# An encoder layer's modulation, projections and attention, reordered

## What is computed

```
mod = silu(c) @ w_ada[l] + b_ada[l]            # 1024 x 6144, six vectors of 1024
h = rms_norm(x, norm1_g[l]) * (1 + sc1) + sh1
z = h @ w_in[l]                                # za 512, zb 768, zq 512, zk 512, zv 512
ya = silu(rms_norm(conv31(val * sigmoid(gate))))   # za: val, gate: the A group
yb = rms_norm(bg * conv3(cg * hv))                 # zb: bg, cg, hv: the B group
yc = diff_attention(zq, zk, zv)                # 4 heads; two softmaxes per head, subtracted
x = x + g1 * (concat(ya, yb, yc) @ w_out[l])
h = rms_norm(x, norm2_g[l]) * (1 + sc2) + sh2
x = x + g2 * ((silu(g) * u) @ w_down[l])       # g, u = halves of h @ w_gate_up[l]
```

## Time and profile before

| | |
|---|---|
| runs (3) | 1303.79, 1305.12, 1305.97 us; median 1305.12 |
| the profiled execution | 1303.42 us, span 1301.7 |
| TensorE busy | 1200.7 us, 92% |
| VectorE, ScalarE, GpSimd busy | 751.9, 459.6, 133.2 us |
| DMA | 158.39 MB, mean 122 GB/s |

### The profile page before, as it was taken

How to read it: one execution, slowest core, us unless ns; L and a number is a source line. 1 busy time by engine, 2 the same in 40 slices (tenths; PEclk the granted TensorE clock), 3 DMA queues, 4 the chain that set the end, 5 groups by cost and what they waited for, 6 DMA issues and landing times.

```text
span 1301.7 us, 14677 instructions
## 1 busy us (share of the span) xinstructions
PE 1200.7 (92%) x5232; PEld 946.1 (73%) x5232; DVE 751.9 (58%) x962; ACT 459.6 (35%) x687; POOL 133.2 (10%) x175
## 2 busy tenths in 40 slices
PE   0799877898999999999999999689899999999999
PEld 0588653486888888888887886337688888888887
DVE  5889988577766433345556898773543333332321
ACT  2323249834322222222224223694332222222220
POOL 6572000031000000001111000001200000000000
PEclk9899999998999999999999999899999999999999
DMA  9552131054766222255552322101222222223232
GB/s 365 188 186 102 65 95 67 1 215 157 247 224 207 85 94 98 95 207 196 194 195 79 97 81 81 49 1 49 81 86 96 95 98 95 96 96 110 100 113 81
DMA packets 39208, 158.39 MB, mean 122 GB/s; under 512 B 4528, under 2 KB 4672, under 8 KB 39040
## 3 DMA queue, kind: packets, MB, share of 16 engines
q1 hardware_dynamic: 29664, 105.02, 24.0%
q0 software_dynamic: 9504, 52.84, 10.8%
HBM read 155.75 MB, written 2.10 MB: 121 GB/s over the span
## 4 chain that ended last, share of the span: by engine, by line
PE 70%; DVE 17%; ACT 5%; POOL 3%; DMA 2%; issue 2%; DVEq 0%; ACTq 0%; SPq 0%; POOLq 0%
PE ps L1174 20%; PE ps L1175 20%; PE ps L1176 20%; DVE uc L880 4%; PE ps L1198 3%; DVE w_lo L804 3%; DVE ada_acc_early L821 2%; PE ps L1346 2%; PE ps L1202 1%; ACT prob L740 1%; DVE ada_acc_first L821 1%; DMA ada_ring_first<-ada 1%; PE ps L1213 1%; DVE neg_max L1061 1%; DMA raw<-w_stream 1%
## 5 line engine op out<-in xcount | busy, mean ns | idle before, releaser
L547 ACT ACTIVATE w_hi<-raw 128x1024 fp32r<-128x1024 f32 x196 | 207.3, 1060 | 674.3 <-PE ps L1176 537.5
L804 DVE TENSOR_TENSOR w_lo<-raw,w_hi 128x1024 fp32r<-128x1024 f32 x196 | 240.8, 1231 | 291.3 <-ACT w_hi L547 289.4
L1174 PE MATMUL ps<-h_hi,w_hi 128*128 128x512 f32 x896 | 349.8, 390 | 0.0
L1176 PE MATMUL ps<-h_lo,w_hi 128*128 128x512 f32 x896 | 349.0, 390 | 0.0
L1175 PE MATMUL ps<-h_hi,w_lo 128*128 128x512 f32 x896 | 349.0, 389 | 0.0
L1174 PEld LDWEIGHTS ps<-h_hi,w_hi 128*128 128x128 f32 x896 | 168.3, 188 | 35.1 <-DVE w_lo L804 0.4
L1176 PEld LDWEIGHTS ps<-h_lo,w_hi 128*128 128x128 f32 x896 | 168.3, 188 | 34.8
L1175 PEld LDWEIGHTS ps<-h_hi,w_lo 128*128 128x128 f32 x896 | 168.3, 188 | 34.6
L1174 PE MATMUL ps<-gu_hi,w_hi 128*128 128x512 f32 x352 | 137.4, 390 | 0.0
L1176 PE MATMUL ps<-gu_lo,w_hi 128*128 128x512 f32 x352 | 137.1, 390 | 0.0
L1175 PE MATMUL ps<-gu_hi,w_lo 128*128 128x512 f32 x352 | 137.1, 390 | 0.0
(11 more groups left out here) (172 smaller groups left out, 1260.0 us busy)
## 6 DMA issues: line engine op xcount, KB each, us to landing
raw<-w_stream SPq DMA_DIRECT2D x196, 512.0 KB, 3.3
ada_ring_late<-ada POOLq DMA_DIRECT2D x16, 768.0 KB, 8.2
ada_ring_first<-ada POOLq DMA_DIRECT2D x12, 768.0 KB, 17.0
ada_ring_gu_hi<-ada POOLq DMA_DIRECT2D x10, 768.0 KB, 5.7
ada_ring_gu_lo<-ada POOLq DMA_DIRECT2D x10, 768.0 KB, 5.1
ada_ring_early<-ada POOLq DMA_DIRECT2D x8, 768.0 KB, 10.1
ada_ring_conv<-ada POOLq DMA_DIRECT2D x4, 768.0 KB, 7.8
xT<-x_t POOLq DMA_DIRECT2D x1, 2048.0 KB, 13.8
```

The costliest lines, as they stand in the source:

```text
L547: act.activation(w_hi[:, u % RING, :], raw[:, u % RAW, :], ACT.Copy).then_inc(s_whi, 1)
L804: dve.tensor_tensor(w_lo[:, u % RING, :], raw[:, u % RAW, :], w_hi[:, u % RING, :].bitcast(F32), ALU.subtract).then_inc(s_wlo, 1)
L1174: pe.matmul(dst, whi, rhs[0][:, n, :], start=start, stop=False)
L1176: return pe.matmul(dst, whi, rhs[1][:, n, :], start=False, stop=stop)
```

## The change

- **Modulation.** w_ada is laid out with its output features on the partitions, so a chunk is one DMA of 512 KB, and its 128 values are row sums: one VectorE operation multiplies 1024 elements by silu(c), which is broadcast over the partitions (`c_b`), and accumulates (`mod_dot`). There are 96 such modulation rows, numbered in the order of use: 0 to 15 are shift and scale 1 of layer 0, from 16 (M_MID) on three for each chunk (gate 1, shift 2, scale 2), from 40 (M_GU) on 28 in gate-up and from 68 (M_DOWN) on 28 in down. TensorE's column sums are gone. Rings hold 8 or 4.
- **Start.** x comes first, in four DMAs of SyncE; the rows follow on GpSimd. The first norm's squares lie in eight buffers and TensorE adds all of them. VectorE computes the angles. Shift and gain of a chunk are made as soon as its two dots are (`first_gain`, on ScalarE).
- **Order.** Units run A (4), K (4), Q (4), V (4), B (6). A and K units hold two chunks of h each; in layer 0 they alternate, chunk by chunk (`a_chunk`, `k_chunk`), in layer 1 A comes before K.
- **B in attention.** A half of a B unit (12 matmuls, `b_half`) stands before the tiles and in each of tiles 0 to 10. Part of the taps (48 operations in layer 0, 26 in layer 1) and the short convolution move to the tiles.
- **Output.** Three units instead of two are taken chunk by chunk, in an order of chunks by layer, and seven banks are in use.

```diff
+N_AK, N_Q, N_V, N_B, N_OUT, N_GU = 8, 4, 4, 6, 8, 2 * FC
...
+A_AT = ((0, 2, 4, 6), (0, 1, 2, 3))
+K_AT = ((1, 3, 5, 7), (4, 5, 6, 7))
...
+TAPS_UNIT = ({9: 1, 10: 2, 13: 1, 14: 2, 15: 1}, {3: 2, 4: 3, 5: 3, 6: 3, 9: 1, 10: 2, 13: 1, 14: 2, 15: 1})
+TAPS_TILE = ([2] * 12, [2] * 6 + [1])
...
+            pool.wait_ge(s_x[1], 16)
+            for m in range(2):
+                ada_load(m)
...
+            pool.wait_ge(s_scores, N_TILES)
+            for m in range(M_MID + 4, M_MID + 8):
+                ada_load(m)
+            for k in range(KC - 1):
+                norm_sum(1, k)
+                for m in range(M_MID + 8 + 3 * k, min(M_MID + 8 + 3 * (k + 1), M_GU)):
+
+                    pool.wait_ge(s_acc, m - 8 + 1)
+                    ada_load(m)
+
+            pool.wait_ge(s_acc, M_GU)
...
+            def first_gain(k):
+
+                act.wait_ge(s_acc, 2 * k + 2)
+                a = mod_at(SH1, k)
+                act.activation(mod[:, 0, a:a + 1], modr[:, 0, a:a + 1], ACT.Identity,
+                               bias=pcol[:, 0, C_BADA + a:C_BADA + a + 1]).then_inc(s_gain0, 1)
+                act.activation(gain[:, 0, 0, k:k + 1], modr[:, 0, a + 1:a + 2], ACT.Identity,
+                               scale=pcol[:, 0, C_N1 + k:C_N1 + k + 1],
+                               bias=n1b[:, k:k + 1]).then_inc(s_gain0, 1)
...
-            def mod_load(G, q, i=0):
-
-                slots, acc = ada_place(G)
-                ada_landed(dve, G, q, i)
-                if q == 0 and G >= FIRST_MG:
-
-                    dve.wait_ge(s_msum, G + i if G in GU_MG else G - 1)
-                for r in range(2):
-                    k = 2 * q + r
-                    src = slots[q][:, r, :]
-                    if k == 0:
-                        dve.tensor_scalar(acc, src, c_act[:, k:k + 1], None, ALU.mult).then_inc(s_acc, 1)
-                    else:
-                        dve.wait_ge(s_acc, 8 * G + k + 8 * i)
-                        dve.scalar_tensor_tensor(acc, src, c_act[:, k:k + 1], acc, ALU.mult,
-                                                 ALU.add).then_inc(s_acc, 1)
...
+            def mod_dot(m):
+
+                ada_landed(dve, m)
+                l, a = divmod(m, MODS)
+                slot = ada_slot(m)
+                dve.scalar_tensor_tensor(slot, slot, 1.0, c_b[:], ALU.mult, ALU.mult,
+                                         accum_out=modr[:, l, a:a + 1]).then_inc(s_acc, 1)
...
+            mod_dot(0)
+            mod_dot(1)
+            dve.wait_ge(s_nrs, 1)
...
+                if l == 0:
+                    for k in range(KC):
+                        dve.wait_ge(s_gain0, 2 * k + 2)
+                        norm_apply(0, 0, k)
+                        if k < 2:
+                            split_lo(2 * k)
+                        elif k + 1 < KC:
+                            mod_dot(2 * k + 2)
+                        norm_lo(0, 0, k)
+                        if k < 2:
+                            mod_dot(2 * k + 2)
+                        if k + 1 < KC:
+                            mod_dot(2 * k + 3)
+                        if k < 2:
+                            split_lo(2 * k + 1)
+                        elif k % 2:
+                            split_lo(k + 1)
+                            split_lo(k + 2)
+                    first = 6
...
+                    taps = TAPS_TILE[l][it] if it < len(TAPS_TILE[l]) else 0
+                    conv_a_taps(l, taps // 2)
+                    row_factors(l, it)
                     if it:
-                        row_mix_in(it - 1)
-                    if 2 <= it < 2 + 2 * CC:
-                        y_lo(l, it - 2)
-                    h, r = divmod(it - 2 * NT, NT)
-                    if h >= 1 and r == 0:
-                        mix_scale(l, 3 + h)
-                    if h >= 1 and r == 3:
-                        y_lo(l, 3 + h)
-                row_mix_in(N_TILES - 1)
+                        row_mix_in(l, it - 1)
+                    for k in range(len(SCALE_AT[l])):
+                        if SCALE_AT[l][k] == it:
+                            mix_scale(l, k)
+                    if it in (2, 6):
+                        short_input(l, it // 4)
+                    if it in (3, 7):
+                        short_conv(l, it // 4)
+                    if it in (8, 10):
+                        short_gate(l, (it - 8) // 2)
+                    conv_a_taps(l, taps - taps // 2)
+                    if it % 2 == 0 and it < 2 * N_B:
+                        split_lo(U + U_B + it // 2 + RING)
...
                 for s in range(N_OUT):
-                    add_to_x(l, s, s % OUT_BANKS, G1, U + U_OUT + s + 1)
+                    if l == 0:
+                        mod_finish(0, M_MID + 3 * s, 3)
+                        dve.wait_ge(s_mod, 3 * (s + 1))
+                    add_to_x(l, s, B_OUT[s], G1, U + U_OUT + s + 1)
                     split_lo(U + U_OUT + s + RING)
-                    if l == 0:
-                        if s == OUT_SUM_AT[0] + 1:
-                            mod_finish(OUT_MG[0])
-                        mods_beside(OUT_MG, OUT_LOADS_AT, s)
+                    if l == 0 and s + 2 < N_OUT:
+                        for m in range(M_MID + 3 * (s + 2), M_MID + 3 * (s + 3)):
+                            mod_dot(m)
                 if l == 0:
-                    mod_finish(OUT_MG[-1])
                     make_gain(0, 1)
-                norm_apply(l, 1)
...
+            def a_chunk(l, u, n):
+
+                r = n % 2
+                pe.wait_ge(s_wlo, u + 1)
+                pe.wait_ge(s_hhi, 2 * KC * l + n + 1)
+                for j in range(2 * CC):
+                    cols = slice(r * T + j * P, r * T + (j + 1) * P)
+                    pe.matmul(ps[:, j, :], w_hi[:, u % RING, cols], h_hi[:, n, :], start=n == 0, stop=False)
+                    pe.matmul(ps[:, j, :], w_lo[:, u % RING, cols], h_hi[:, n, :], start=False, stop=False)
+                pe.wait_ge(s_h, 2 * KC * l + n + 1)
+                for j in range(2 * CC):
+                    cols = slice(r * T + j * P, r * T + (j + 1) * P)
+                    mm = pe.matmul(ps[:, j, :], w_hi[:, u % RING, cols], h_lo[:, n, :], start=False,
+                                   stop=n == KC - 1)
+                if r:
+                    mm.then_inc(s_unit, 1)
...
-            for g in range(FIRST_MG - 1):
-                mod_sum(g)
-            norm_stat(0)
-            mod_sum(FIRST_MG - 1)
+            pe.wait_ge(s_const, 1)
+            for k in range(KC):
+                pe.wait_ge(s_sq, k + 1)
+                mm = pe.matmul(ps[:, B_STAT, :], ones[:], sq0[:, k, :], start=k == 0, stop=k == KC - 1)
+            mm.then_inc(s_nstat, 1)
...
+                if l == 0:
+                    for n in range(KC):
+                        a_chunk(l, U + A_AT[l][n // 2], n)
+                        k_chunk(U + K_AT[l][n // 2], n)
+                else:
+                    for n in range(KC):
+                        a_chunk(l, U + A_AT[l][n // 2], n)
+                    for n in range(KC):
+                        k_chunk(U + K_AT[l][n // 2], n)
...
+                def b_half(i):
+
+                    u = U + U_B + i // 2
+                    pe.wait_ge(s_wlo, u + 1)
+                    if i == 0:
+                        pe.wait_ge(s_v, NT * l + 1)
+                    elif i in (2, 6):
+                        pe.wait_ge(s_cg, CC * l + i // 4 + 1)
+                    elif i in (4, 8):
+                        pe.wait_ge(s_hb, CC * l + i // 4)
+                    elif i == 10:
+                        pe.wait_ge(s_short, N_SHORT * l + CC * TAPS_B + 1)
+                    for n in range(4 * (i % 2), 4 * (i % 2) + 4):
+                        mm = product(ps[:, B_B, :], u % RING, n, h, n, n == 0, n == KC - 1)
+                    if i % 2:
+                        mm.then_inc(s_unit, 1)
...
+                b_half(0)
                 scores(0)
                 scores(1)
                 for it in range(N_TILES):
+                    if it % 2 == 0 and it < 2 * N_B:
+                        b_half(it + 1)
                     if it + 2 < N_TILES:
                         scores(it + 2)
...
+                    if it % 2 and it + 1 < 2 * N_B:
+                        b_half(it + 1)
...
+                w_out_part(0, 3)
                 weights_t(N_TILES - 1)
-                mix_stat(l, HEADS)
-                w_out_pair(2, 3)
+                w_out_part(3, 5)
+                mix_stat(l, 4)
                 attend(HEADS - 1, 0, NT)
-                w_out_pair(3, 4)
-                mix_stat(l, HEADS + 1)
-                w_out_pair(4, KC)
-
-                for s in range(2, N_OUT):
-                    if s >= OUT_BANKS:
-
-                        pe.wait_ge(s_xnew, 2 * KC * l + s - OUT_BANKS + 1)
-                    unit(U + U_OUT + s, s % OUT_BANKS, h, order)
-                    if l == 0 and s in OUT_SUM_AT:
```

(4 more changed lines are left out.)

1322 lines of the change are left out of this document (661 added, 661 removed).

## The result

The changed kernel takes **1334.24 us** (1332.43 to 1336.32), the kernel before 1305.1 beside it: ratio **1.0229** (95% interval 1.0214 to 1.0245). Forecast were 1291, with 1266 to 1315 as the range. The profiled execution has a span of 1330.9 us. The milestones on TensorE, which answer: first product, first scores, fourth output unit and gate-up of layer 0, then start, fourth output unit and gate-up of layer 1.

A forecast was written before the change was run, and what follows sets the result against it. TensorE was taken to bound plain matrix work, with time lost at the start, column sums and attention. Layer 0 to gate-up +1.5, sums -11.3, layer 1 -0.5 and -2: -12.3 on 1303.42 gives 1291 us, range 1266 to 1315.

The forecast's parts named there:

- the ring of the tiles: Attention tiles 0 to 11: TensorE, ScalarE, VectorE wait in turn, 12.0 us per pair; 75 us layer 0, 72 layer 1.
- 13 + 28 + 2: Layer 1's end of attention: 13 us for tiles 12 to 15, 28 from last tile to T, 2 added.
- The certain part: Feed-forward of layer 0: all TensorE column sums go, 11.3 us saved; a dot of 1024 should take 1.28 us.
- The start: Start of layer 0: first product at 19 us (17 to 24) instead of 47.9, eight units done at 71.
- Q and V: Stretch up to attention: layer 0's attention starts at 127 instead of 201, layer 1's 96.5 us after that layer's start.
- T: Point where three output units of a layer are done; forecast 252 in layer 0, 902 (892 to 914) in layer 1.
- The output stage: Layer 0's output stage: six steps of 8.8 us, each waiting for a load behind a sum; 23 us lost.
- T0: Layer 0's point with three output units done: forecast 252 us (240 to 262), against 273.7 before.
- rival 2: Layer 0's output stage: loads early enough, stage at TensorE's 5.46 us, 27 us less, 1264 us; chance 0.10.
- costs nothing in my sum: Layer 0's output stage: the dot held 1.0 us by GpSimd's sum isn't the one waiting for the load, so adds 0.
- rival 3: Layer 0's output stage: same ring with slow loads, each step pays its landing, 1323 us at worst; chance 0.17.
- rival 4: Start of layer 0: VectorE late by 12 us, products begin early but are starved, 1303 us; chance 0.08.

The follow-up runs named there:

- e13: The changed kernel with 30 useless TensorE matmuls added where its attention waits for long, no order changed: 1321.45 us, ratio 1.0126.
- e8: The kernel with e1 and e2 together, with layer 1's silu of the convolution output one tile earlier, in tile 10: 1291.03 us, ratio 0.9903.
- e1: The changed kernel with GpSimd issuing the modulation loads of layer 0's output stage ahead of the sums of squares: 1319.36 us, ratio 1.0126.
- e11: The kernel of e8 with the seven sums of squares of layer 0's output stage on VectorE instead of GpSimd: 1286.04 us, ratio 0.9871.
- e2: The changed kernel with ScalarE's and VectorE's weight steps in attention one tile later, behind the odd tile's exponentials and mixing: 1312.08 us, ratio 1.0063.
- e9: The changed kernel with all taps of a tile behind its mixing on VectorE, same operations in another order: 1318.02 us, ratio 1.0110.

## Why the prediction was wrong, step by step

The likeliest case, 1291 us and so 14 us faster, fell; the kernel is 29 us slower. Two steps of the prediction carry most of the miss: the ring of the tiles, priced with TensorE at full clock ("75 us for twelve tiles", and 72 in layer 1), and layer 1's last four tiles and tail ("13 + 28 + 2").

**The certain part: right.** From gate-up of layer 0 to layer 1 took 366.8 us, before 379.5: 12.7 us less, forecast 11.3 and 0.5. The dot takes 1.22 us (forecast 1.28).

**The start: right in kind, 5.5 us late.** First product at 24.5, forecast 19 (17 to 24). The eight sums of squares were given no price: they are sixteen passes that take TensorE from 9.5 to 19.4, the first seven of them at half pace (below), while ScalarE had its last square ready at 13.4. Eight units were done at 75.5 (71).

**Q and V: right.** First row maximum at 134.5, forecast 127, of which 4.5 us are the start's. Layer 1: 98.6 us after its start, forecast 96.5.

**Attention with half units: here it failed.** The step "12.0 us per pair and 12.9 with the attended product: 75 us for twelve tiles" gave the unit 5.46 us at full clock. The ring was right, and right in length but for the clock: from the end of a unit to the next transposes it had 6.0 us, the pair above shows 6.75; for TensorE's part it had 6.95, the pair shows 9.65. Twelve tiles took 80.4 us, and the five long units of layer 0 alone took 7.3 us more than 5 x 5.46. e13, with a clock of 0.95, took 74.8, the 75 of the forecast. The text did see a lower clock, but in the output stage alone, where it costs nothing, and not in the ring of which TensorE is a part. Layer 1 took 78.7 us, forecast 72; e13 took 76.1. The rest there is ScalarE's queue: behind the last unit w_hi, two rstd operations, a copy and a square (3.3 us) stand ahead of the next exponentials, and the forecast had counted these statistics from tile 12 on only.

```profile
870.56 1.06 ACT L497 ACTIVATE w_hi<-raw 128x1024 fp32r<-128x1024 f32 x1 [4.81 <-PE ps L1217]
871.52 0.67 ACT L631 ACTIVATE rstd<-ps,eps 128x512 f32<-128x512 f32 x1
...
873.37 0.63 ACT L622 ACTIVATE work_b<-oc 128x512 f32<-128x512 f32 x1
873.90 0.67 ACT L577 ACTIVATE prob<-ps,neg_max 128x512 f32<-128x512 f32 x1
```

**Tiles 12 to 15 and the tail.** Up to the end of the last row maximum, tiles 12 to 15 took 15.5 us in layer 0 (14) and 21.0 in layer 1 (13). The silu with its two table loads was added for layer 0 only; e8 shows 3.6 us for it in these tiles of layer 1 (4.7 by the ratios). From the last tile to T: 38.0 us (36) and 36.5 (30). To the first addition it was 37.8 and 36.2, and in e13, at a clock of 1.00 in both, 35.7 and 33.2. The 3 us left in layer 1 may be the three units by chunk that stand ahead of the last tile's transposes on TensorE (two units before); that is argued and wasn't tried. The forecast's bases were weak here too. Its own terms for tiles 12 to 15, four at 3.2 us and 4.5 above, make 17.3 and not 14. And from the end of the last row maximum to T the kernel before took 30.8 us, not 28, after 10.9 for its tiles 12 to 15. The stretch from tile 12 to T was thus 41.7 us before, 50 and 43 in the forecast, 53.5 and 57.5 measured: in layer 1 the forecast added 1.3 us to the old kernel's time, and 15.8 came. These 14.5 us are the largest single miss.

**The output stage: right, and hardly too short.** Six round trips, 8.95 us each on average (8.8), T0 to gate-up 63.5 us (60.5). Landing plus issue of the load that ends a step: 270.88 to 275.19, 4.3 us; the forecast had 4.2. By the fit of the Trainium skill (DMA: Bandwidth & Descriptors, Anatomy of one DMA — SWDGE (gpsimd) path) the landing would be 3.2, an estimate; the measured 4.3 stands above it. What the forecast had wrong is what lies under the trip: it gave rival 2, early loads, TensorE's pace and 27 us, and e1 found 13.4, with VectorE as the bound at 6.5 us a step. There the dot beside GpSimd's sum, "costs nothing in my sum", costs 1.1 us each time; e11 removes it for 0.68 us of VectorE's own sum, and a step falls by 0.5.

**The sum.** Layer 0 up to gate-up: +19.4 us above the forecast (7.5 to attention, 5.4 and 1.5 tiles, 2.0 tail, 3.0 output stage). Feed-forward: -0.9. Layer 1 up to T: +23.3 (2.0, 6.7, 8.0, 6.5). Together 41.8, on 1291.1: 1332.9, and the profiled execution took some 1332.7. No rival had it: rival 3 (slow landings) ends on the same side by another mechanism, rival 4 (a starved start) had the place of 7 of these us. One cause is common to four terms (tiles and tails of both layers), each estimated at full clock; e13 gives the clock 13.4 of the 42 us (good to about 3). Its matmuls also cost time and the clock stays below 1.00 in its tiles, so the share is more likely larger than smaller. The rest has other causes: the passes of the start (5.5), the silu (3.6), the landings (3.0), ScalarE's queue in layer 1, the weak bases above and an excess over the ring that none of the runs takes apart. Since e2 and e9 shorten idle stretches and so raise the clock as well, their gains overlap with it, and how much of the miss is order alone is not separated further.

## What to carry to other kernels

When independent TensorE work is put between the tiles of a chain through other engines, ask of each other engine's queue what stands between "unit done" and the tile's next link; whatever waits for the unit (the next weights, gates) goes behind the chain's own link, and filler work there goes into the time in which TensorE is busy. Price TensorE's part of such a chain at both clock levels where it waits about 3 us at a time, as here, even if its work increases. A load whose issue stands in one queue behind a sum of the step that needs it makes a round trip of the whole step; with the loads ahead, look what is the bound below before counting the gain.

## What the runs showed of the hardware

A dot of 1024 with an accumulator takes 1.22 us. In e1, started 0.3 us after a GpSimd sum of 1.53 us it took 2.32, and without the sum (e11) it took 1.22 again. The Trainium skill (SBUF — State Buffer, SBUF: two separate sides) has this as an exclusive lock, and the trace agrees: the 1.23 us left of the sum and the 1.22 of a dot make 2.45, close to the 2.32.

TensorE's clock fell to its lower level in idle stretches of 2.2 to 3.3 us: five times in the twelve tiles of layer 0, a stage in which it was busy for 61.07 of 80.5 us. Before, it was busy for 22.29 of 30 us in the same tiles, idle 1.9 us once and then at most 1.0 us at a time, and the clock stayed at 1.00. That more work came with a lower clock I had not expected.

At the start TensorE ran at half pace in a stretch for which the clock is given as 1.00: the first seven passes start 0.85 to 0.98 us apart, those from 15.4 on 0.43 (as such passes do at full clock elsewhere). The trace has no record of the clock before 15.2 us, so the 1.00 is not a reading there. At 0.43 all sixteen would have taken 6.9 us in place of 9.9.

```profile
9.50:13.00 3.50, 3.49 (x4) 1.49 (x5) 3.33 (x14) 3.29 (x7) 2.05 (x4) 1.00 1.02 419
13.00:19.50 6.50, 6.42 (x13) 2.53 (x11) 6.26 (x11) 0.43 (x1) 4.12 (x13) 1.00 1.02 410
```
